# Four transposes into an unused bank in front of the strips of the third norm's mean

## What is computed

```python
def rms_norm(x, g):
    xf = x.astype(jnp.float32)
    y = xf * lax.rsqrt(jnp.mean(xf * xf, axis=-1, keepdims=True) + RMS_EPS)
    return (y * g.astype(jnp.float32)).astype(x.dtype)

def swiglu(h, w_gate, w_up, w_down):
    return (jax.nn.silu(h @ w_gate) * (h @ w_up)) @ w_down
...
        x = x + 0.5 * swiglu(rms_norm(x, norm_ffn1[l]), ffn1_gate[l], ffn1_up[l], ffn1_down[l])
...
        x = x + merged @ w_out[l]
        x = x + 0.5 * swiglu(rms_norm(x, norm_ffn2[l]), ffn2_gate[l], ffn2_up[l], ffn2_down[l])
    return rms_norm(x, norm_final)
```

## Time and profile before

| | |
|---|---|
| median of 3 runs | 610.37 us (609.87 to 612.18) |
| the profiled execution | 609.67 us |
| its span, first to last instruction | 607.9 us |
| TensorE busy, matmuls | 599.8 us, 99% |
| VectorE busy | 411.4 us, 68% |
| ScalarE busy | 300.4 us, 49% |
| mean rate of the DMA | 173 GB/s |
| mean granted TensorE clock | 0.999 |

### The profile page before, as it was taken

The page is one execution under the profiler, slowest core; times in us unless marked ns, Lnnn a source line. Parts: engine busy times, 40 slices in busy tenths (PEclk is TensorE's granted clock), DMA queues, the critical chain, the costliest instruction groups (busy, mean ns, idle before and its releaser), DMA issues.

```text
span 607.9 us, 14875 instructions
## 1 busy us (share of the span) xinstructions
PE 599.8 (99%) x6490; PEld 584.0 (96%) x6490; DVE 411.4 (68%) x495; ACT 300.4 (49%) x355; POOL 75.7 (12%) x85
## 2 busy tenths in 40 slices
PE   9999999999999999999999999999999999999996
PEld 8999999999999899989988989999999999999996
DVE  5866887775556469979883347878766666665552
ACT  6634664444444274445656446646544444443341
POOL 1016800000003000033216433000000000000000
PEclk9999999999999999999999999999999999999999
DMA  9867665555667245585442233459765556556601
GB/s 305 267 189 232 207 200 181 182 179 193 193 196 235 71 140 181 186 213 120 136 140 73 76 110 101 138 170 287 237 205 182 178 194 207 187 175 198 197 4 70
DMA packets 100736, 105.39 MB, mean 173 GB/s; under 512 B 2276, under 2 KB 98828, under 8 KB 100692
## 3 DMA queue, kind: packets, MB, share of 16 engines
q1 hardware_dynamic: 99380, 101.47, 52.3%
q0 software_dynamic: 1152, 3.02, 2.2%
q10 hardware_dynamic: 160, 0.27, 0.1%
HBM read 103.50 MB, written 1.25 MB: 172 GB/s over the span
## 4 chain that ended last, share of the span: by engine, by line
PE 98%; DMA 1%; issue 0%; DVE 0%; SPq 0%; DVEq 0%; ACT 0%
PE two L1596 27%; PE two L1597 26%; PE two L1598 26%; PE two L1592 15%; PE two L1941 1%; DMA x_tok<-in_x 1%; PE two L1885 1%; PE two L1887 1%; PE two L1886 1%; PE two L1858 0%; PE two L1739 0%; PE two L1859 0%; PE two L1994 0%; PE two L1860 0%; DVE out_tok L1582 0%
## 5 line engine op out<-in xcount | busy, mean ns | idle before, releaser
L988 DVE TENSOR_TENSOR w_lo<-w_raw,w_hi 128x2048 fp32r<-128x2048 f32 (+1 forms) x68 | 154.3, 2269 | 68.0 <-ACT w_hi L567 48.5
L1596 PE MATMUL two<-hlo_f,w_hi 128*128 128x256 f32 x640 | 176.9, 276 | 0.0
L1597 PE MATMUL two<-hhi_f,w_lo 128*128 128x256 f32 x640 | 176.7, 276 | 0.0
L1598 PE MATMUL two<-hhi_f,w_hi 128*128 128x256 f32 x640 | 176.6, 276 | 0.0
L567 ACT ACTIVATE w_hi<-w_raw 128x2048 fp32r<-128x2048 f32 (+1 forms) x53 | 100.4, 1895 | 134.1 <-PE two L1598 116.9
L1596 PEld LDWEIGHTS two<-hlo_f,w_hi 128*128 128x128 f32 x640 | 120.1, 188 | 0.8 <-issue 0.8
L1597 PEld LDWEIGHTS two<-hhi_f,w_lo 128*128 128x128 f32 x640 | 120.1, 188 | 0.0
L1598 PEld LDWEIGHTS two<-hhi_f,w_hi 128*128 128x128 f32 x640 | 120.1, 188 | 0.0
L1598 PE MATMUL two<-hid_hi_t,w_hi 128*128 128x256 f32 x352 | 97.2, 276 | 0.0
L1596 PE MATMUL two<-hid_lo_t,w_hi 128*128 128x256 f32 x352 | 97.2, 276 | 0.0
L1597 PE MATMUL two<-hid_hi_t,w_lo 128*128 128x256 f32 x352 | 97.2, 276 | 0.0
(11 more groups left out here) (359 smaller groups left out, 1025.4 us busy)
## 6 DMA issues: line engine op xcount, KB each, us to landing
w_raw<-in_w_in SPq DMA_DIRECT2D x20, 1024.0 KB, 5.1
w_raw<-in_ffn_gate SPq DMA_DIRECT2D x15, 1024.0 KB, 5.3
w_raw<-in_ffn_up SPq DMA_DIRECT2D x15, 1024.0 KB, 5.3
w_raw<-in_ffn_down SPq DMA_DIRECT2D x12, 896.0 KB, 4.9
w_raw<-in_ffn_down SPq DMA_DIRECT2D x6, 1024.0 KB, 5.2
h_f<-in_ffn_gate SPq DMA_DIRECT2D x5, 1024.0 KB, 5.4
out_tok<-in_ffn_up SPq DMA_DIRECT2D x5, 1024.0 KB, 5.2
w_raw<-in_w_out SPq DMA_DIRECT2D x4, 1024.0 KB, 5.4
```

Source lines behind the costliest of these rows:

```text
L988: nc.vector.tensor_tensor(wlo[slot][:, 0:kts], (raw[slot] if buf is None else buf)[:, 0:kts], whi[slot][:, 0:kts].bitcast(F32), ALU.subtra ...
L1596: mm(dst, whi[slot][:, k_, cols], xl, start=start, stop=False)
L1597: mm(dst, wlo[slot][:, k_, cols], xh, start=False, stop=False)
L1598: return mm(dst, whi[slot][:, k_, cols], xh, start=False, stop=stop)
```

## The change

```diff
@@ -1690,6 +1690,8 @@
                     late_pair(bank[0], 0, hhi_f, hlo_f, "hlo_ready", 4 * q + 1).then_inc(sg["multiplied"], 1)
                     pe.wait_ge(sg["first_lo"], 8)
                     pe.wait_ge(sg["up_taken"], g0)
+                    for j in range(4):
+                        nc.tensor.transpose(bank[7][:, j * P:(j + 1) * P], x[:, j // 2, j % 2 * P:(j % 2 + 1) * P], ident)
                     mean_square(q)
                     for m in range(2):
                         for c in range(KD):
```

## The result

The changed kernel takes a median of 617.05 us over 8 runs (612.44 to 618.98), the kernel before 610.50 over its 8 (609.87 to 612.18). The ratio is 1.0073, 95% interval 1.0047 to 1.0099: slower by 0.7%, clear of the noise. The median hides the shape. The eight times are 612.44, 612.51, 612.58 and 616.60, 617.49, 617.71, 617.78, 618.98: **two groups**, with nothing in between, at a granted clock of 0.998 to 0.999 in each. Together with two later runs of the same kernel (`a_copy` and `a_look`), 25 of 32 executions are in it; of the kernel before, run beside all experiments, 10 of 147.

A forecast was written before the change was run, and what follows sets the result against it. The prediction took TensorE, busy 99%, as the bound. Its terms summed to 0.44 us, taking the profiled 609.67 to 610.11; with the runs' median 0.70 above the profile, the forecast was 610.8 us, range 609.9 to 612.9.

The forecast's parts named there:

- What bounds the kernel: TensorE, busy 99% of the span: whatever is put into its stream is paid in full unless it falls into a hole.
- Term 1: Four transposes between the gate chunk's last matmul and the strips: distance 0.65 instead of 0.21, costing 0.44 us.
- Term 2: Waits for up weights and free bank move onto the first transpose; all are met before 424.29: cost 0.
- Term 3: ScalarE's root to VectorE's line 988, behind the strips: it moves with TensorE by 0.44, slack stays 0.24: cost 0.
- Term 4: SyncE's weight loads issue at most 0.44 us later, with TensorE's need later by the same: cost 0.
- Term 5: Rhythm of the 1536 wide matmuls behind the strips: stays at 113.3 ns, cost 0; at 117.8 ns 6.9 us.
- A: The wide stretch behind the strips falls into 117.8 ns and keeps it: 6.9 + 0.44 us, median about 617.7; 12%.
- B: A wait behind the strips, ScalarE over 0.24 late, delays the next gate chunk: 0.2 to 1 us more; 2%.
- C: The transposes in front of the strips cost nothing, filling a hole or standing elsewhere: median 610.4; 2%.
- D: The granted clock falls to 1.2 GHz around the transposes and long stretch; about 5 us there makes 0.5%; 1%.
- E: The new entry brings the wide stretch a rhythm under 113.3 ns; 112 would give 2 us; 2%.
- The forecast's own case: Only the four transposes cost, 0.44 us, with the wide stretch kept at 113.3 ns: 610.8 us; 81%.

The follow-up runs named there:

- a_copy: The changed kernel run again without further change: median 618.53 us, 11 of 12 executions at 616 us or more; its profiled execution took 617.08 us.
- a_look: The changed kernel run a third time, for its profile and share: median 617.65 us, 9 of 12 executions at 616 us or more.
- one_T: The changed kernel with one transpose instead of four in front of the strips: median 612.51 us, 5 of 12 executions at 616 us or more.
- behind: The kernel before with the four transposes put behind the strips, not in front: median 611.41 us, 0 of 12 executions at 616 us or more.
- both: The kernel before with four transposes in front of the strips and four more behind them: median 611.33 us, ratio to before 1.000.
- eight_T: The changed kernel with eight transposes instead of four in front of the strips: median 618.32 us, 6 of 6 executions at 616 us or more.
- front_gate: The kernel before with the four transposes in front of the gate chunk, not the strips: median 612.02 us, 0 of 12 executions at 616 us or more.
- before_118: The kernel before with four products of attention's form (64-column weights) in front of the gate chunk: median 611.73 us, 1 of 12 at 616 us or more.
- wide_then_T: The changed kernel with four wide matmuls ahead of the four transposes: median 618.39 us, 10 of 12 executions at 616 us or more.
- spread_in: The changed kernel with four products of 32-row weights and 512 columns in front of the gate chunk: median 612.95 us, 3 of 12 at 616 us or more.

## Why the prediction was wrong, point by point

*What bounds the kernel: right.* TensorE's stream is paid in full, and the whole loss lies in it.

*Term 1, the four transposes: right.* 0.65 from matmul to strips, 0.44 more than before, in the first profile; the same in `a_copy` (424.45 to 425.09, 0.64). The 81 ns for a matmul of 128 columns in the page "TensorE: Matmul & The Clock Gate" of the Trainium skill (section Back-to-back issue gap), an estimated 0.32 for four, fits neither.

*Term 2, the waits that move: right.* No profile has a hole between the gate chunk and the up chunk.

*Term 3, the train behind the strips: right for the transposes, too calm about the place.* The slack stayed 0.24, and in the changed kernel nothing was lost there. But 0.24 is the distance between an end and a start that depends on it, and it was hardly any slack: in `one_T`, a matmul stream that opens 0.01 us quicker than before's (425.24 to 425.69, where before has 425.07 to 425.53) comes to it with 227 ns and is held up. Behind that it loses not 0.02 us but the rhythm of the 1488 matmuls that follow. I had priced a slip there at 0.16 us; the upper group of `one_T` has a median of 616.6 against 611.0 below.

*Term 4, the ring: right.* No hole in the long stretch in the profiles of either group: behind 434 us no two starts are more than 0.12 apart.

*Term 5, the rhythm: this step failed.* Its price was right, 6.9 us forecast and 6.8 measured, and so was the reading that a wrong rhythm stays. Wrong was "what stands directly in front seems to set it, and that stays as it is". The strips alone do not set it: by the shares above, the same strips lead to 113 behind wide matmuls nearly always and to 118 three times of four behind transposes. The term that I took as 0 was 6.82 us in the profile of `a_copy`. The five places of five that I counted had strips behind five different things, and only one of these had transposes; there the strips have 128 columns, not 256. And one trace is one draw of each place: it showed each place's outcome once, and I took that as certain.

*The rivals.* A, with 12%, happened in 25 executions of 32 by the times. Its reason, that the choice hangs on a few nanoseconds at the entry, fits the traces: the spacings behind the first one are 119, 116, 114 in before and 117, 118, 118 in `a_copy`. The 262 cycles that I had set against it stand in the Trainium skill (the same page and section) for a matmul by itself, not for a stream, and so said nothing on it. B, C and D did not happen: no wait behind the strips, the transposes do cost their 0.44, the clock stayed at 1.00. E did not either.

*What the numbers should have been.* With two outcomes 7 us apart and one new sequence between them, the range had to reach to 618 unless A could be excluded; five of five from one execution does not exclude it. The forecast's own case, 610.8, lies near what `behind` (611.41) and `both` (611.33) measured.

## What to carry to other kernels

When a long stretch of one kind of matmul follows an edit, look at the spacing of its starts, not only at holes, busy share and clock: 4.5 ns on each of 1500 matmuls is 1% and shows in none of the three, only in a recorded duration of 281 instead of 276. Put a change of form in front of such a stretch only with several executions in hand, and look at all their times: two groups with a gap say that one profile is not enough. Where such a stretch has to be entered from another form, try another last form; here four idle transposes behind the strips removed the loss for 0.4 us.

## What was not expected of the hardware

- One instruction has two steady spacings at a granted clock of 1.00: 113.3 and 117.8 ns for 128x128 weights and 256 columns. Either lasts over 1500 matmuls, through the branches of two loops and through semaphores already met.
- Which one comes up differs between executions of one program, with shares that belong to the sequence of forms (upper group, by the times): strips behind wide matmuls 10 of 147, behind four transposes 25 of 32, transposes last 0 of 24.
- It can turn in the middle: `one_T` turned at one matmul, behind a delay of some 0.02 us in all, for the rest of the kernel, and `eight_T` behind one of 0.014, while stalls of 0.013 and 0.012 at the same matmul in `front_gate` and `before_118` were followed by the 113 rhythm again. What tells these apart is open, as is what physically has the two phases; no run here separates it.
- A load of 1 MB of the output projection that lands late goes with a gap of 0.4 to 1.0 us between two starts at the same matmul in seven of the seventeen later profiles and in the first one of the change, and with one of 0.16 to 0.22 in three more; before has none. ScalarE's wait for that load is 3.0 to 3.9 us in these profiles and 2.6 to 2.8 in those without the gap. Behind this gap too either rhythm follows, 118 in five of the eleven and 113 in six, and not by its length: 0.97 was followed by 113 in `wide_then_T`, 0.16 by 118 in `spread_in`. What else differs between executions lies further ahead: the merge products start between 377.7 and 381.1 in all profiles.
